# Turning the operands of fp32 split products: weights stationary, 256 tokens moving, in a two-layer decoder trunk

## The chip, the core and the metric

The kernel runs on one core of a Trainium2 chip. The core has TensorE (matmuls, results only into PSUM), VectorE (DVE), ScalarE (ACT), GpSimd (POOL) and SyncE (SP), which here issues the loads. The metric is the device time of one execution, in microseconds, as the median of several runs. Before the change it is 2340.84 us (three runs, 2338.79 to 2340.88).

## The reference

256 tokens of width 2048 go through two layers, all in fp32.

```
mod = silu(c) @ ada_w + ada_b            # shift, scale, gate; six vectors of 2048 a layer
h = x * (1 + scale) + shift
layer 0: y = gated linear attention(h)   # keys, queries (1024 each), values, r (2048 each),
                                         # gate logits of rank 16, chunks of 64 tokens, 4 heads;
                                         # o = rmsnorm(o) * g * silu(r), then @ w_out
layer 1: y = stick-breaking attention(h) # q from h, k and v from x, 16 heads, then @ w_out
x = layernorm(alpha * x + (1 + gate) * y)
y = relu(h @ w1 + b1)^2 @ w2 + b2        # the MLP of both layers, 2048 -> 8192 -> 2048
x = layernorm(alpha * x + (1 + gate) * y)
```

## The kernel before

**Weights.** All weight matrices come as 768 tiles of 128 x 1024 fp32 (512 KB) in one fixed order, into a ring of four slots (`raw`). ScalarE writes the rounded high part `w_hi` (L320), DVE the rest `w_lo = raw - w_hi` (L678). The activations are split the same way, into `h_hi` and `h_lo`, with the model width on partitions and the tokens along the columns. A product is then three matmuls of the type fp32r: w_hi with h_hi (L1071), w_hi with h_lo (L1072), w_lo with h_hi (L1075). Other matmuls (attention, transposes) are plain fp32.

**Two kinds of tiles.** A *stripe* is eight tiles that hold 512 output columns and all 2048 input rows, two blocks of 128 rows in a tile. `stripe_tile` makes h the stationary operand (128 tokens) and 512 weight columns the moving one: 2 blocks x 2 token halves x 3 = 12 matmuls of 512 columns in a tile. The results stand with tokens on partitions in two PSUM banks; stripes alternate between banks 0, 1 and banks 2, 3 (`par`). The *wide* tiles (`wide`) serve the projections back to width 2048 (`go`, `d0`, `ao`, `d1`); they have 12 matmuls of 512 columns too and are not changed.

The stages in order, with their tiles: lead 24 (half of the queries and all keys of layer 0, loaded beside the first modulation rows), gq1 8 (the other queries), gv 32, gr 32, go 32, u0 128, d0 128, aq 32, ak 32, av 32, ao 32, u1 128, d1 128.

**Results turned afterwards.** Keys, queries and the MLP's hidden layer are wanted with output columns on partitions. So after a stripe ScalarE copies its two banks to `S` (`rows_out`, L344), TensorE transposes them in eight blocks of 128 x 128 into banks 6 and 7 (`turn`, L1109), and ScalarE (`relu` L357, `keep_turned` L365) or DVE (`gla_keys`, `gla_queries`) takes them from there. DVE squares the relu's result (L956). A new stripe waits until the copy of the stripe before the last is done (`rows_copied`).

**Order.** Nothing is scheduled by the hardware. Each engine's block is a list of tiles, and a hook table `H[tile]` says which small operations follow which tile; the loops of the MLPs pass their hooks by tile number within two stripes. ScalarE and DVE split tile t as soon as slot t - 4 has been used, so they can be up to three tiles ahead of TensorE.

**Modulation vectors.** 200 + 24 rows of 128 x 2048 weights (1 MB) are multiplied on DVE with the broadcast silu(c) and summed (L683), spread over the stages.

**Gate rows.** The residual (L742, L743) multiplies y, which has tokens on partitions, with 1 + gate along the columns, the same for all partitions. `gate_column` makes the gate as a 128 x 16 column block; `gate_spread` (L1144) transposes each of its columns, broadcast to 128 x 128, so that 16 transposes make the rows in PSUM, eight at a time; `gate_rows` (L412) copies them to `G`. This happens four times.

**The gate of r.** silu(r) is built from functions of one table set: on ScalarE Abs (L541), Exp, Ln and Exp, on DVE two operations between and after them, then `o_gate` multiplies o with it. Heads of o go through the same two banks 4 and 5 one after another (`o_head`, L1232).

**Stage ends.** Before the next stage DVE adds the residual, makes mean and variance and normalises; TensorE transposes X (L1122) to make the next h.

Of the kernel before, what the change touches and what calls it, by code (L numbers as in the profile page):

```python
# [66 lines left out]
STRIPE0 = {"gv": 4, "u0": 8, "aq": 24, "ak": 28, "av": 32, "u1": 36}  # L67
TURNED0 = {"u0": 4, "aq": 20, "ak": 24, "u1": 28}
# [8 lines left out]

GLAO_AT = [T0["gr"] + i for i in (24, 25, 26, 27, 31)] + [T0["go"] + i for i in (0, 7, 8)]
# [5 lines left out]
def build_kernel(nc, tiles, mods, c_t, x_rows, mod_b, ln_t, b1_t, bg_t, w_gl, wgu, normg_t, ln_rows, b2_rows, out):  # L84
# [3 lines left out]
    with ctx:  # L88
# [55 lines left out]
        gla_rows = [rows_buf, G[:, 0:TW], G[:, TW:2 * TW], rows_buf]  # L144
# [27 lines left out]
        rows_copied, blocks_turned = sem("rows_copied"), sem("blocks_turned")  # L172
        turned_act, turned_dve, squared = sem("turned_act"), sem("turned_dve"), sem("squared")
        src_hi, src_lo = sem("src_hi"), sem("src_lo")
        g_made, g_spread, g_copied = sem("g_made"), sem("g_spread"), sem("g_copied")
# [5 lines left out]
        r_ln, r_log, r_sig, part_done = sem("r_ln"), sem("r_log"), sem("r_sig"), sem("part_done")  # L181
# [4 lines left out]

        block = ctx.enter_context(nc.Block())

        def h_bank(occ, pr):
            return {H_GLAO: 6 + pr % 2, H_KV: 4 + pr % 2}.get(occ, 4 + pr % 4)  # L190

# [66 lines left out]
        def _(pool):  # L258
# [35 lines left out]

            pool.wait_ge(h_lo_ready, PAIRS * (H_GLAO + 1))
            load_rows(0)
            load_b2(0)
            pool.wait_ge(tile_used, T0["d0"] + 128)
            load_rows(1)
            pool.wait_ge(a_exp, SB_H // 2)  # L300
            load_rows(2)
            load_b2(1)
            pool.wait_ge(tile_used, T0["d1"] + 64 + 32)
# [4 lines left out]
        def _(act):  # L308
# [30 lines left out]
            def rows_out(done, par, dst, s=None):  # L339
                def f():  # L340
                    act.wait_ge(tile_used, done)
                    if s is not None:
                        act.wait_ge(blocks_turned, s)
                    nc.scalar.activation(dst, ps[:, 2 * par:2 * par + 2, :], ACT.Copy).then_inc(rows_copied, 1)  # L344
                return f
# [16 lines left out]
            def keep_turned(s, dst, scale=1.0):  # L362
                def f():
                    act.wait_ge(blocks_turned, s + 1)
                    nc.scalar.activation(dst, ps[:, 6:8, :].rearrange("p a n -> p (a n)"), ACT.Copy, scale=scale)\  # L365
                      .then_inc(turned_act, 1)
                return f
# [38 lines left out]
            def gate_rows(occ, r):  # L406
                def f():
                    bank = GATE_BANK[occ]
                    if occ == 0:
                        act.wait_ge(blocks_turned, N_GLA_TURNED)  # L410
                    act.wait_ge(g_spread, 2 * occ + r + 1)
                    nc.scalar.activation(G[:, r * TW:(r + 1) * TW], ps[:, bank:bank + 2, :].rearrange("p a n -> p (a n)"), ACT.Copy)\  # L412
                      .then_inc(g_copied, 1)
                return f
# [81 lines left out]
            rows3 = lambda v: v.rearrange("p (a n) -> p a n", a=TOK)  # L496

            for j, (bank, dst) in enumerate(((2, gla_rows[1]), (0, gla_rows[0]), (4, gla_rows[2]))):
                def f(j=j, bank=bank, dst=dst):
                    act.wait_ge(tile_used, K - LEAD_TILES + j + 1)  # L500
                    nc.scalar.activation(rows3(dst), ps[:, bank:bank + 2, :], ACT.Copy).then_inc(rows_copied, 1)
                H[K + j].append(f)
            for at, f in ((4, gate_log), (5, gate_log2), (6, gate_log3), (9, decays1), (10, decays2), (12, decays3)):
                H[K + at].append(f)
            H[K + 14].append(rows_out(K + 8, 1, rows3(gla_rows[3]), 1))
# [10 lines left out]
            def o_squares(h):  # L516
                def f():
                    act.wait_ge(o_done, h + 1)
                    for tok in range(TOK):
                        link(nc.scalar.activation(o_junk, ps[:, 4 + tok, :], ACT.Square, accum_out=ssq[:, 2 * h + tok:2 * h + tok + 1]))  # L520
                return f

            def o_out(h):
                def f():
# [3 lines left out]
                    for tok in range(TOK):  # L528
                        ins = nc.scalar.activation(gO[:, tok, h * GLA_DV:(h + 1) * GLA_DV], ps[:, 4 + tok, :], ACT.Identity,
# [4 lines left out]
            def r_abs(i):  # L534
                def f():
# [3 lines left out]
                    else:  # L539
                        act.wait_ge(blocks_turned, N_GLA_TURNED)  # L540
                    link(nc.scalar.activation(staged(), ps[:, 2 * (i % 2):2 * (i % 2) + 2, :], ACT.Abs))  # L541
                return f

            def r_exp(i):
                return lambda: link(nc.scalar.activation(rows_buf, rows_buf, ACT.Exp, scale=-1.0))

            def r_log1p(i):
                return lambda: nc.scalar.activation(rows_buf, rows_buf, ACT.Ln, bias=1.0).then_inc(r_ln, 1)

            def r_gate(i):  # L550
                def f():
                    act.wait_ge(r_log, i + 1)
                    nc.scalar.activation(rows_buf, rows_buf, ACT.Exp).then_inc(r_sig, 1)
                return f

            for h in range(GLA_H):
                B = RR + 8 * h
                for at, f in ((7, o_squares), (8, o_out), (11, r_abs), (12, r_exp), (13, r_log1p), (15, r_gate)):
# [907 lines left out]
```

## Time and profile before

| | |
|---|---|
| median of three runs | 2340.84 us (2338.79 to 2340.88) |
| the profiled execution | 2337.4 us |
| its span | 2335.6 us |
| instructions in the span | 31124 |
| TensorE busy | 2264.4 us, 97% of the span |
| DVE busy | 1753.2 us, 75% |
| ScalarE busy | 1142.1 us, 49% |
| mean DMA rate | 280 GB/s |
| mean granted TensorE clock | 0.985 of full speed |

Busy shares are averages over stages with different limits. Matmuls overlap in the records: a record of 0.39 us can start every 0.23 us, so the time that a matmul costs is read from start to start or from the chain of waits, not from its mean. A weight load (PEld) is a record of its own beside the matmuls. The span runs from the first instruction to the last; the execution's own time holds 1.8 us more.

### The profile page before, as it was taken

Reading aid. Unit: us, or ns where it says so; the run is one execution under the profiler, and the core shown is the slowest. Engines: PE = TensorE matmul, PEld = TensorE weight load, DVE = VectorE, ACT = ScalarE, POOL = GpSimd, SP = SyncE. Lnnn points to the kernel's source line nnn. Section 1 sums busy time; section 2 is a strip of 40 time slices with the busy share of each in tenths; the row PEclk is TensorE's granted clock in tenths of the full one; section 3 lists DMA queues with packets and bytes.
Section 4 is the critical chain, followed back from the end, with each engine's and each line's share of the span. In section 5 each row is a group of like instructions: output and inputs, shape, how many; then the busy total and the mean of one; then the engine's idle time right before and its main releaser. Section 6 shows DMA issues by size and latency. Waiting matters only on the chain.

```text
span 2335.6 us, 31124 instructions
## 1 busy us (share of the span) xinstructions
PE 2264.4 (97%) x10288; PEld 1863.1 (80%) x10288; DVE 1753.2 (75%) x1679; ACT 1142.1 (49%) x1379; POOL 14.5 (1%) x34
## 2 busy tenths in 40 slices
PE   5799999999999999999999999999999999999997
PEld 3578878778888888888878888887888888888886
DVE  6989788897777788898896975679765445556656
ACT  3354466364444555444455555545444445444442
POOL 1000000000000000000000000000000000000000
PEclk8899999999999999999999999999999999999999
DMA  9979888879888888979978865676776555666563
GB/s 388 399 295 364 330 323 303 322 286 340 332 314 331 322 337 336 337 255 349 339 297 309 303 249 198 251 286 236 273 281 220 188 180 180 212 193 191 196 227 125
DMA packets 145689, 653.91 MB, mean 280 GB/s; under 512 B 16400, under 2 KB 16656, under 8 KB 115520
## 3 DMA queue, kind: packets, MB, share of 16 engines
q1 hardware_dynamic: 144000, 642.05, 75.2%
q0 software_dynamic: 1600, 10.69, 1.2%
q8 instruction: 54, 0.88, 0.2%
q14 instruction: 35, 0.29, 0.0%
HBM read 650.57 MB, written 2.10 MB: 279 GB/s over the span
## 4 chain that ended last, share of the span: by engine, by line
PE 90%; DVE 5%; DMA 2%; issue 1%; ACT 0%; SPq 0%; DVEq 0%; ACTq 0%
PE ps L1071 28%; PE ps L1072 28%; PE ps L1075 28%; DMA R<-in_mods 2%; PE ps L1109 2%; DVE w_lo L678 1%; PE ps L1122 1%; DVE mod_w L683 1%; DMA mod_w<-in_mods 1%; DVE X L743 1%; DVE stats L745 0%; DVE S L742 0%; PE ps L1216 0%; PE ps L1232 0%; DVE R L683 0%
## 5 line engine op out<-in xcount | busy, mean ns | idle before, releaser
L678 DVE TENSOR_TENSOR w_lo<-raw,w_hi 128x1024 fp32r<-128x1024 f32 x768 | 934.4, 1222 | 530.0 <-ACT w_hi L320 500.8
L1071 PE MATMUL ps<-w_hi,h_hi 128*128 128x512 f32 x3072 | 1216.5, 396 | 0.0
L1072 PE MATMUL ps<-w_hi,h_lo 128*128 128x512 f32 x3072 | 1204.0, 392 | 0.0
L320 ACT ACTIVATE w_hi<-raw 128x1024 fp32r<-128x1024 f32 x768 | 810.2, 1059 | 756.9 <-PE ps L1075 680.0
L1075 PE MATMUL ps<-w_lo,h_hi 128*128 128x512 f32 x3072 | 828.7, 390 | 2.3 <-DVE w_lo L678 2.3
L1071 PEld LDWEIGHTS ps<-w_hi,h_hi 128*128 128x128 f32 x3072 | 581.9, 189 | 125.9 <-issue 5.5
L1075 PEld LDWEIGHTS ps<-w_lo,h_hi 128*128 128x128 f32 x3072 | 578.2, 188 | 124.7 <-DVE w_lo L678 3.1
L1072 PEld LDWEIGHTS ps<-w_hi,h_lo 128*128 128x128 f32 x3072 | 581.9, 189 | 118.6 <-issue 0.7
L683 DVE SCALAR_TENSOR_TENSOR mod_w<-mod_w,cs 128x2048 f32<-128x2048 f32 x200 | 456.7, 2284 | 14.1 <-ACT cs L436 8.4
L976 DVE TENSOR_TENSOR h_lo<-R,h_hi 128x512 fp32r<-128x512 f32 x128 | 87.6, 684 | 10.7 <-ACT h_hi L588 10.7
L357 ACT ACTIVATE S<-ps,b1t 128x256 f32<-128x256 f32 x128 | 50.2, 475 | 85.5 <-PE ps L1109 85.5
L588 ACT ACTIVATE h_hi<-R 128x512 fp32r (+1 forms) x128 | 78.7, 615 | 0.0
L344 ACT ACTIVATE S<-ps 128x1024 f32<-128x1024 f32 x41 | 42.2, 1028 | 65.1 <-PE ps L1075 64.4
L447 ACT ACTIVATE R<-R,coef 128x256 f32<-128x256 f32 x16 | 8.7, 593 | 76.7 <-DVE coef L838 76.7
L1194 PE MATMUL ps<-R 128*16 128x256 f32 x32 | 11.7, 506 | 34.5 <-DVE h_lo L819 34.5
L1109 PEld LDWEIGHTS ps<-ident,S 128*128 128x128 f32 x336 | 39.2, 140 | 5.5
L1109 PE MATMUL ps<-ident,S 128*128 128x128 f32 x336 | 43.5, 272 | 0.0
L683 DVE SCALAR_TENSOR_TENSOR R<-R,cs 128x2048 f32<-128x2048 f32 x16 | 36.5, 2286 | 7.4 <-DMA R<-in_mods 7.4
L956 DVE TENSOR_TENSOR R<-S 128x1024 f32 (+1 forms) x32 | 39.0, 1218 | 0.0
L1122 PE MATMUL ps<-ident,X 128*128 128x128 f32 x160 | 25.7, 304 | 13.1 <-DVE X L756 12.2
L381 ACT ACTIVATE S<-ps,coef 128x256 f32<-128x256 f32 x64 | 32.3, 555 | 10.2 <-PE ps L1122 7.7
L1122 PEld LDWEIGHTS ps<-ident,X 128*128 128x128 f32 x160 | 21.4, 157 | 18.0 <-DVE X L756 13.8
(146 smaller groups left out, 629.9 us busy)
## 6 DMA issues: line engine op xcount, KB each, us to landing
raw<-in_tiles SPq DMA_DIRECT2D x768, 512.0 KB, 4.4
mod_w<-in_mods SPq DMA_DIRECT2D x200, 1024.0 KB, 6.7
R<-in_mods SPq DMA_DIRECT2D x16, 1024.0 KB, 10.8
R<-in_ln_rows POOLq DMA_DIRECT2D x8, 1024.0 KB, 8.1
G<-in_mods SPq DMA_DIRECT2D x4, 1024.0 KB, 10.7
S<-in_mods SPq DMA_DIRECT2D x4, 1024.0 KB, 12.7
X<-in_x_rows SPq DMA_DIRECT2D x1, 2048.0 KB, 11.2
S<-in_b_rows POOLq DMA_DIRECT2D x2, 1024.0 KB, 7.5
```

Source lines behind the costliest of these rows:

```text
L320: nc.scalar.activation(w_hi[:, slot, :], raw[:, slot, :], ACT.Copy).then_inc(hi_ready, 1)
L344: nc.scalar.activation(dst, ps[:, 2 * par:2 * par + 2, :], ACT.Copy).then_inc(rows_copied, 1)
L357: ins = nc.scalar.activation(turned_buf[:, blk * SEQ:(blk + 1) * SEQ], ps[:, 6 + blk // 2, (blk % 2) * SEQ:(blk % 2 + 1) * SEQ], ACT.Relu, ...
L588: nc.scalar.activation(h_hi[:, slot:slot + 2, :], R[:, bass.ds(kt * SEQ, 2 * SEQ)].rearrange("p (a t) -> p a t", a=2), ACT.Copy).then_inc( ...
L678: nc.vector.tensor_tensor(w_lo[:, slot, :], raw[:, slot, :], w_hi[:, slot, :].bitcast(F32), ALU.subtract)\
L683: nc.vector.scalar_tensor_tensor(buf, buf, 1.0, cs[:], ALU.mult, ALU.mult, accum_out=mod_t[:, bass.ds(a, 1)]).then_inc(mod_done, 1)
L976: nc.vector.tensor_tensor(h_lo[:, slot:slot + 2, :], R[:, bass.ds(kt * SEQ, 2 * SEQ)].rearrange("p (a t) -> p a t", a=2), h_hi[:, slot:slo ...
L1071: mm(dst, h_hi[:, kt, toks], w_hi[:, slot, c], start=start, stop=False, skip_group_check=more)
L1072: return mm(dst, h_lo[:, kt, toks], w_hi[:, slot, c], start=False, stop=False, skip_group_check=more)
L1075: return mm(dst, h_hi[:, kt, tok * P:(tok + 1) * P], w_lo[:, slot, c], start=False, stop=stop, skip_group_check=more)
L1109: last = nc.tensor.transpose(ps[:, 6 + blk // 2, o:o + P], rows[:, tok * SW + blk * P:tok * SW + (blk + 1) * P], ident[:])
L1122: last = nc.tensor.transpose(ps[:, h_bank(occ, pr), i * SEQ + tok * P:i * SEQ + (tok + 1) * P], src[:, tok, kt * P:(kt + 1) * P], ident[:])
```

## The change

- A new `turned_tile` takes the place of `stripe_tile` for the lead, gq1, u0, aq, ak and u1 (352 tiles). The stationary operand is a block of 128 weight columns, the moving one h with all 256 tokens: 2 row blocks x 4 column blocks x 3 = 24 matmuls of 256 columns in a tile. Results stand with output columns on partitions, four blocks of 256 tokens in the same two banks.
- `turn` and the copies ahead of it are gone; relu and `keep_turned` read the stripe's own banks after `tile_used`, one step in place of two. Keys and queries of layer 0 are copied once and read by DVE from `S` and `G`. A stripe waits for `turned_act` of the stripe two before in place of `rows_copied`. DVE's squares move from tiles 15 and 7 to tiles 13 and 5.
- `gate_spread` and `gate_rows` are gone. `gate_turn` makes one transpose of the 128 x 16 block, ScalarE copies the 16 x 128 result, POOL stores it in DRAM and loads it back broadcast to all partitions (`spread_gate`). The residual waits for that load.
- The gate of r is one Silu, with the other table loaded again afterwards. The o products move from tiles 3, 11, 19, 27 of stage gr to tiles 3, 5, 8, 10 and alternate between two pairs of banks.
- values, r and the wide tiles keep their products.

```diff
+            def turned_tile(t, j, par, inputs=None, slot=None, bank=None):
+                pe.wait_ge(hi_ready, t + 1)
+                if inputs is not None:
+                    pe.wait_ge(h_lo_ready, inputs)
+                slot = j % RING if slot is None else slot
+                bank = 2 * par if bank is None else bank
+                parts = [(2 * (j % ST) + i, ps[:, bank + blk // 2, (blk % 2) * SEQ:(blk % 2 + 1) * SEQ],
+                          slice(i * SW + blk * P, i * SW + (blk + 1) * P), blk % 2 == 0) for i in range(2) for blk in range(SW // P)]
+
+                for kt, dst, c, clears in parts:
+                    mm(dst, w_hi[:, slot, c], h_hi[:, kt, :], start=kt == 0 and clears, stop=False, skip_group_check=True)
+                    mm(dst, w_hi[:, slot, c], h_lo[:, kt, :], start=False, stop=False, skip_group_check=True)
+                pe.wait_ge(lo_ready, t + 1)
+                for kt, dst, c, _ in parts:
+                    last = mm(dst, w_lo[:, slot, c], h_hi[:, kt, :], start=False, stop=kt == KT - 1, skip_group_check=True)
+                last.then_inc(tile_used, 1)
...
-            def relu(s, i, layer, first=False):
+            def relu(done, par, i, layer, first=False):
                 def f():
-                    act.wait_ge(blocks_turned, s + 1)
+                    act.wait_ge(tile_used, done)
                     if not (first and layer == 0):
                         act.wait_ge(squared, 16 * layer + i)
                     for blk in range(4):
                         col = 64 * layer + 4 * i + blk
-                        ins = nc.scalar.activation(turned_buf[:, blk * SEQ:(blk + 1) * SEQ], ps[:, 6 + blk // 2, (blk % 2) * SEQ:(blk % 2 + 1) * SEQ],
+                        ins = nc.scalar.activation(turned_buf[:, blk * SEQ:(blk + 1) * SEQ],
+                                                   ps[:, 2 * par + blk // 2, (blk % 2) * SEQ:(blk % 2 + 1) * SEQ],
                                                    ACT.Relu, bias=b1t[:, bass.ds(col, 1)])
...
+            def gate_turn(occ):
+                def f():
+                    pe.wait_ge(g_made, occ + 1)
+                    if occ == 0:
+                        pe.wait_ge(o_copied, 3)
+                    elif occ != 2:
+                        pe.wait_ge(turned_act, TURNED0["u0" if occ == 1 else "u1"] + 16)
+                    nc.tensor.transpose(ps[0:KT, GATE_BANK[occ], 0:P], g_col[:], ident[:]).then_inc(g_turned, 1)
...
+            def spread_gate(occ):
+                pool.wait_ge(g_kept, occ + 1)
+                pool.dma_start(g_rows[occ, :, :], G[0:KT, 0:P]).then_inc(g_stored, 16)
+                pool.wait_ge(g_stored, 16 * (occ + 1))
+                pool.dma_start(G[:].rearrange("p (k n) -> p k n", k=KT), g_rows[occ, :, :].unsqueeze(0).to_broadcast([P, KT, P]))\
+                    .then_inc(g_loaded, 16)
...
-                stripes(up, u, occ, hooks(0, first=True))
+                stripes(up, turned_tile, lambda k: None, occ, {j: [f] for j, f in enumerate(rest)})
                 with pe.Fori(1, 8) as b:
-                    stripes(up + BODY * b, u + 2 * b, None, hooks(b))
+                    stripes(up + BODY * b, turned_tile, lambda k: pe.wait_ge(turned_act, s + 2 * b + k - 1), None, {})
...
+O_AT = [T0["gr"] + i for i in (3, 5, 8, 10)]
+SILU_AT = [T0["gr"] + i for i in (16, 19, 27, 35)]
...
+                    nc.scalar.activation(staged(), ps[:, 2 * (i % 2):2 * (i % 2) + 2, :], ACT.Silu).then_inc(r_taken, 1)
```

## Rows read from the trace of the kernel before

**Rows 1.** The page, its part on the chain that ended last: shares of the span.
```profile
PE 90%; DVE 5%; DMA 2%; issue 1%; ACT 0%; SPq 0%; DVEq 0%; ACTq 0%
PE ps L1071 28%; PE ps L1072 28%; PE ps L1075 28%; DMA R<-in_mods 2%; PE ps L1109 2%; DVE w_lo L678 1%; PE ps L1122 1%; DVE mod_w L683 1%; DMA mod_w<-in_mods 1%; DVE X L743 1%; DVE stats L745 0%; DVE S L742 0%; PE ps L1216 0%; PE ps L1232 0%; DVE R L683 0%
```
**Rows 2.** Waits of the whole run: who for whom, us in total, times, longest.
```profile
ACT w_hi L320 <- PE ps L1075: 680.0, 494, 3.4
...
PE ps L1194 <- DVE h_lo L819: 34.5, 8, 13.2
...
PE ps L1075 <- DVE w_lo L678: 2.3, 2, 1.4
```
**Rows 3.** Waits of SyncE's queue, 487 to 851 us.
```profile
SPq L211 <- DVE w_lo L678: 267.9, 125, 4.8
```
**Rows 4.** Stretches: length, busy us (instructions) of PE, PEld, DVE, ACT, POOL, clock, DMA, GB/s.
```profile
0.00:143.00 143.00, 101.33 (x371) 71.97 (x372) 115.64 (x121) 51.59 (x70) 9.18 (x24) 0.86 0.96 378
...
258.00:354.00 96.00, 96.00 (x421) 76.52 (x420) 77.72 (x71) 56.21 (x74) 0.00 (x0) 1.00 0.92 349
...
487.00:851.00 364.00, 364.00 (x1672) 302.59 (x1671) 289.72 (x254) 176.43 (x214) 0.00 (x0) 1.00 0.86 324
```
**Rows 5.** Chain of waits, 555 to 601 us: start, us, what.
```profile
562.31 0.91 PE ps L1075 x4
...
565.03 0.91 PE ps L1075 x4
...
576.82 0.87 PE ps L1109 x8
...
599.50 0.87 PE ps L1109 x8
```
**Rows 6.** Groups by line, TensorE, shapes apart: busy us, mean ns, idle before.
```profile
L1109 PE MATMUL ps<-ident,S 128*128 128x128 f32 x336 | 43.5, 272 | 0.0
...
L1144 PE MATMUL ps<-ident,g_col 128*128 128x128 f32 x64 | 8.3, 272 | 0.0
...
L1109 PE MATMUL ps<-ident,G 128*128 128x128 f32 x16 | 2.1, 272 | 0.0
```
**Rows 7.** Chain of waits, 1436.5 to 1440.5 us, two attention products of heads.
```profile
1437.37 0.43 PE ps L1375 x2
1437.81 0.22 PE ps L1376 x2
```
**Rows 8.** Groups by line, weight loads, shapes apart.
```profile
L1376 PEld LDWEIGHTS ps<-R 128*128 128x128 f32 x32 | 6.1, 189 | 0.8
```
**Rows 9.** Instructions in order of time, all engines, 1363.2 to 1363.6 us.
```profile
1363.22 0.19 PEld L1071 LDWEIGHTS ps<-w_hi,h_hi 128*128 128x128 f32 x1
...
1363.33 0.19 PEld L1072 LDWEIGHTS ps<-w_hi,h_lo 128*128 128x128 f32 x1
...
1363.56 0.39 PE L1072 MATMUL ps<-w_hi,h_lo 128*128 128x512 f32 x1
```
**Rows 10.** TensorE in order of time, 61.2 to 63.4 us, slow clock at first.
```profile
61.24 0.63 PE L1071 MATMUL ps<-w_hi,h_hi 128*128 128x512 f32 x1
61.67 0.63 PE L1072 MATMUL ps<-w_hi,h_lo 128*128 128x512 f32 x1
```
**Rows 11.** TensorE in order of time, last products before a stop (69.49 to 73.86 us).
```profile
69.26 0.61 PE L1075 MATMUL ps<-w_lo,h_hi 128*128 128x512 f32 x2
```
**Rows 12.** TensorE in order of time, 1437 to 1440 us.
```profile
1436.76 0.61 PE L1075 MATMUL ps<-w_lo,h_hi 128*128 128x512 f32 x2
```
**Rows 13.** ScalarE in order of time, 577.77 to 600.45 us, relu of one stripe.
```profile
577.91 1.57 ACT L357 ACTIVATE S<-ps,b1t 128x256 f32<-128x256 f32 x4 [2.72 <-PE ps L1109]
```
**Rows 14.** Stretches, one stripe of the up projection of layer 0.
```profile
577.77:600.45 22.68, 22.68 (x106) 18.84 (x104) 17.30 (x16) 10.87 (x13) 0.00 (x0) 1.00 0.86 322
```
**Rows 15.** ScalarE in order of time, 0 to 14 us.
```profile
0.80 1.28 ACT L429 ACT_TABLE_LOAD   x1 [0.80 <-PEq L1456]
```
**Rows 16.** The page, DMA issues: count, KB each, us to landing.
```profile
R<-in_ln_rows POOLq DMA_DIRECT2D x8, 1024.0 KB, 8.1
```

More of the change, by code:

```diff
@@ L539, in f @@
                     else:
[L540 to L553, printed above, removed]
+                        act.wait_ge(turned_dve, N_GLA_TURNED)
+                    nc.scalar.activation(staged(), ps[:, 2 * (i % 2):2 * (i % 2) + 2, :], ACT.Silu).then_inc(r_taken, 1)
                 return f
             for h in range(GLA_H):
[L557 to L561 removed]
+                H[O_AT[h] + 4].append(o_squares(h))
+                H[O_AT[h] + 5].append(o_out(h))
+                H[SILU_AT[h]].append(r_silu(h))
+            H[SILU_AT[GLA_H - 1] + 1].append(lambda: nc.scalar.preload_act_table_set("natural_log_exp_and_others"))
+            H[RR + 17].append(gate_row_out(0))
             for pr in range(PAIRS):
@@ L569, in mlp @@
             def mlp(layer):
-                up, down, s = T0[f"u{layer}"], T0[f"d{layer}"], TURNED0[f"u{layer}"]
+                up, down = T0[f"u{layer}"], T0[f"d{layer}"]
                 def hooks(b, first=False):
                     i, t = 2 * b, up + BODY * b
-                    late = {10: [rows_out(t + 8, 0, staged(), s + i)], 14: [relu(s + i, i, layer, first)]}
-                    early = {2: [rows_out(t, 1, staged(), s + i - 1)], 6: [relu(s + i - 1, i - 1, layer)]}
+                    late = {11: [relu(t + 8, 0, i, layer, first)]}
+                    early = {3: [relu(t, 1, i - 1, layer)]}
                     return late if first else {**late, **early}
@@ L599, in mlp @@
                     t = down + 64 * half
-                    extra = {2: [rows_out(down, 1, staged(), s + 15)], 6: [relu(s + 15, 15, layer)],
-                             12: [gate_rows(1 + 2 * layer, 0)], 15: [gate_rows(1 + 2 * layer, 1)]} if half == 0 else {}
+                    extra = {3: [relu(down, 1, 15, layer)], 12: [gate_row_out(1 + 2 * layer)]} if half == 0 else {}
                     body(t, src_hooks(t, 0, extra, made=4))
@@ L997, in mlp @@
                     if half == 0:
-                        extra = {7: [square(15)], 8: [lambda: gate_column(1 + 2 * layer, f"g_m{layer}")]}
+                        extra = {5: [square(15)], 8: [lambda: gate_column(1 + 2 * layer, f"g_m{layer}")]}
                     else:
@@ L1091, in _, with stripes @@
             H = defaultdict(list)
-            def stripes(t, u, occ=None, hooks=None):
+            def stripes(t, tile, free, occ=None, hooks=None):
                 for j in range(BODY):
                     if j % ST == 0:
-                        pe.wait_ge(rows_copied, u + j // ST - 1)
-                    stripe_tile(t + j, j, j // ST, None if occ is None or j >= ST else PAIRS * occ + j + 1)
+                        free(j // ST)
+                    tile(t + j, j, j // ST, None if occ is None or j >= ST else PAIRS * occ + j + 1)
@@ L1198, in _ @@
                     t = LEAD_TILES * pr + i
-                    stripe_tile(t, pr, None, slot=t % RING, bank=bank)
+                    turned_tile(t, pr, None, slot=t % RING, bank=bank)
             def gates():
@@ L1324, in _ @@
                 H[Q + j].append(f)
[L1325 to L1329 removed]
+            H[Q + 18].append(gate_turn(2))
             def turn_kv(pr):
@@ L1383, in _ @@
                 H[HEAD_AT[p]].append(head_part(p))
-            for i in range(6):
-                stripes(Q + BODY * i, u + 2 * i, {0: H_Q, 2: H_KV}.get(i))
+            for i in range(4):
+                stripes(Q + BODY * i, turned_tile, lambda k, s=TURNED0["aq"] + 2 * i: pe.wait_ge(turned_act, s + k - 1), {0: H_Q, 2: H_KV}.get(i))
+            stripes(V, stripe_tile, lambda k: pe.wait_ge(turned_act, TURNED0["ak"] + 3 + k))
+            stripes(V + BODY, stripe_tile, lambda k: pe.wait_ge(rows_copied, STRIPE0["av"] + 1 + k))
             heads = lambda j: (head_lo, j // 2 + 1)
```

175 lines of the change are left out of this document (59 added, 116 removed).

## The prediction

> **What bounds the kernel now.** I read the chain of waits first: it is 90% TensorE, and three lines of split products (L1071, L1072, L1075) hold 28% each [rows 1]. Then the waits, for what feeds it late. Over the whole run matmuls wait 34.5 us for h_lo, all of it in the lead, and for the weights' low part (w_lo) only 2.3 us; ScalarE waits 680 us for TensorE, so it runs ahead [rows 2]. In the up projection of layer 0 alone SyncE waits 267.9 us for a free slot before it loads, so loads run ahead too [rows 3]. The stretches show TensorE busy all of 258 to 354 us and 487 to 851 us, DVE at 80% [rows 4]. Outside the lead (0 to 143 us, where loads rule) and the four stage ends, time is therefore the sum of TensorE's instructions. The chain gives their prices [rows 5]. Four split products take 0.91 us, 0.2267 each; 12 of them are one tile, which repeats at 2.72 us (562.31 to 565.03). A stripe of 8 tiles and one group of eight transposes repeats at 22.68 (576.82 to 599.50); 8 x 2.72 = 21.76 leaves 0.92 us for the group, of which its own piece is 0.87.
>
> **Transposes of results: removed.** 336 + 16 = 352 of them [rows 6], 44 groups: 4 in the GLA part, 32 in the MLPs, 8 for queries and keys. None lies in the lead. 44 x 0.92 = 40.5 us off the path.
>
> **Gate rows: 64 transposes of a broadcast column [rows 6] become 4 of a 128x16 block.** Eight groups of 0.92, less four single transposes at about 0.15 (an eighth of 0.87, and the 0.05 that a change of kind takes around a group): 7.4 - 0.6 = 6.8 us.
>
> **The turned product decides.** A tile had 12 products of 512 moving columns; it gets 24 of 256, each with a weight load of its own. The columns streamed are the same, the instructions double. The trace has no split product of 256 columns, so neighbours bound it.
> - Weight load. Two plain fp32 matmuls of 128 columns, each with a load of 128, take 0.22 us, 0.11 each, though a load's record lasts 189 ns [rows 7, 8]: such a load repeats every 0.11 us and hides beside the other's stream. Two loads of split products stood 0.11 apart as well (1363.22, 1363.33), and from the first of them to the second product are 0.34 us, 0.227 of which is the first product: 0.11 to 0.115 [rows 9]. That is just about half of 0.2267.
> - Stream. At 2.4 GHz 512 columns would be 213.3 ns; the chain has 226.7, so 13.3 over. At a granted clock of 1.2 GHz they step by 0.43 (61.24, 61.67), which is 512 / 1.2 with nothing over [rows 10]. Plain fp32 of 256 columns takes 0.43 for two, 0.215 each, two passes of 106.7 with 2 ns over [rows 7]. So 13 ns arise only where 4-byte columns stream at the full rate. If they belong to the stream (a rate limit of 16/17), 256 columns cost 113.3; if to the instruction, 106.7 + 13.3 = 120.0. The last two products before a stop, the very last with no load behind it, make a record of 0.61 us [rows 11]; two with a load behind them also 0.61 [rows 12]. So the next load isn't what stretches them.
> I take the stream: 113.3, a tile of 24 x 0.1133 = 2.72 us as before, cost zero. The ends are 0.109 (an eighth of a group, 0.87) and 0.124 (rival C).
> The Trainium skill (TensorE: Matmul & The Clock Gate, section Back-to-back issue gap) has a rule against the change: a warm matmul lasts N/2.4 plus about 2.5 ns, the latter for each instruction whatever its size. By that 12 more instructions a tile cost 0.03 us. The rule gives 215.8 for 512 columns where the row has 226.7, so it is not the whole price of a split product; what it would do here is rival G.
>
> **Eviction.** A copy of the stripe, then relu from turned banks, becomes one relu (four pieces, 1.57 us [rows 13]) straight from the stripe's banks. ScalarE has 10.87 us of a stripe's 22.68 [rows 14]: nothing on the path. A stripe now waits until the stripe two before is evicted; that comes after tile 3 of the one between, 4 tiles (11 us) ahead: nothing. With that cover gone each stripe would pay the 1.57.
>
> **DVE, DMA.** A stripe shrinks to 21.76 us; DVE has 17.30 in it [rows 14], 80%, with the square now two tiles earlier. The up projection moved 324 GB/s and would ask for 338; 349 was held at 258 to 354 us [rows 4]. Nothing; at worst the pace stays and its 16 groups, 14.7 us, are lost (rival D).
>
> **Silu gate.** Per head Abs, Exp, Ln, Exp on ScalarE and two DVE operations become one Silu. It needs another table, so two loads at 1.28 each [rows 15]. ScalarE is busy 56 of 96 us there [rows 4] and TensorE doesn't wait for it. Nothing; uncovered, 2.6 us. The o products of heads 1 to 3 come earlier, in banks of their own: the same instructions. Their squares and scalings (about 3 us a head) now fall into ScalarE's tiles 7 to 15 of the stage, 12 + 9 splits of 1.1 = 22 us against 24.5 of TensorE, which waits for the second head's at the earliest 3 tiles later.
>
> **Gate rows by DRAM.** POOL issues an 8 KB store and a broadcast load of 1 MB, each behind the copy out of PSUM. The nearest 1 MB load on that queue takes 8.1 us [rows 16]; I double it for store and wait: 16. Readers come 39 tiles (106 us) later in the GLA part and over 50 later elsewhere. Behind them in POOL's queue stand only the norm and bias rows, due a stage later. Nothing.
>
> **Lead.** Its 24 tiles are turned too, beside loads; the products wait there [rows 2]. Nothing. The stage ends keep their chain.
>
> **Sum.** The profiled execution took 2337.4 us (span 2335.6 and 1.8 around it): 2337.4 - 40.5 - 6.8 = 2290.1. The median of the runs shown, 2340.84, is 3.4 above it: 2294.
>
> **Rivals.**
> - *B, the 13.3 ns are paid per instruction.* 24 x 0.120 = 2.88, 0.16 more a tile, on 328 tiles (352 turned less 24 in the lead) +52.5; less 47.3 is +5.2: 2346, slower. The change loses from 113.3 + 47300 / (328 x 24) = 119.3 ns a product. For it: 226.67 ns are exactly 256 + 16 ticks of 1.2 GHz as well as 17/16 of 256. Against: [rows 10 to 12]. Chance 0.26.
> - *C, the weight load doesn't hide.* If the 13.3 come on top of a load of 0.11, a product takes 0.124: +0.26 a tile, +84, net +37: 2378. Against: the fp32 pairs [rows 7], but those stream their columns at half the rate. 0.11.
> - *D, loads or DVE hold the up projection of layer 0 at its pace*: 14.7 less: 2308. Against: [rows 3]. 0.08.
> - *E, at 256 columns the excess vanishes*: 0.109, a tile 2.62, 34 us more: 2260. For it only the fp32 pairs. 0.05.
> - *G, a small fixed part beside the rate.* If 2.5 of the 226.7 are per instruction, as fp32 has 2 over, 256 columns take 112.1 + 2.5 = 114.6: 0.03 a tile, +10: 2304. 0.17.
>
> **Numbers.** The forecast holds 0.33, 2294, its own range 2286 to 2302. Such timing tells 0.2%, 4.7 us. Faster: 0.33 + 0.17 + 0.08 + 0.05 = 0.63. B lies at the line (2342 to 2350 with its joins): 0.11 as same, 0.15 as slower; with C slower is 0.26. The range leaves out E and C and holds B: 2280 to 2352.
>
> **What would show it.** Turned products in the up projection starting every 113 ns (mine), 115 (G), 120 (B), 124 (C) or 109 (E); its 16 tiles in 43.5 us, in B 46.1; no transposes between stripes; down projections unchanged at 2.72 us a tile; TensorE busy throughout with waits for w_lo of a few us. A gap ahead of each stripe, products waiting for w_lo, or a residual waiting for G would show me wrong elsewhere.

## The result

The changed kernel takes 2343.56 us (median of 20 runs, 2341.40 to 2346.41); the kernel before took 2338.81 beside it (20 runs, 2336.15 to 2343.18). The ratio is 1.0018 [1.0011, 1.0025]: 4.7 us slower (2.6 to 5.8), a small amount, but clear of the noise. The forecast was 2294. The time is that of rival B (2346, net +5.2), and the turned products start every 120 ns, which is B's price.

The profiled execution took 2341.98 us, with a span of 2340.3. The chain of waits, by engine and by line, answers to [rows 1]. L1056, L1057 and L1060 are the old products of 512 moving columns; L1086, L1087 and L1090 are the turned ones of 256 (w_hi with h_hi, w_hi with h_lo, w_lo with h_hi).

```profile
PE 87%; DVE 7%; DMA 3%; issue 2%; ACT 0%; SPq 0%; DVEq 0%; ACTq 0%
PE ps L1060 15%; PE ps L1056 15%; PE ps L1057 15%; PE ps L1086 13%; PE ps L1087 13%; PE ps L1090 13%; DVE w_lo L683 2%; DMA R<-in_mods 2%; DVE mod_w L688 1%; DMA mod_w<-in_mods 1%; PE ps L1111 1%; DMA raw<-in_tiles 1%; DVE X L748 1%; DVE S L747 1%; DVE stats L750 1%
```

The waits of the whole run (who for whom, us in total, times, longest) answer to [rows 2]. ScalarE still waits for TensorE, not the other way round; TensorE's waits for h_lo and w_lo are as before in sum; the new wait of POOL for its own DRAM store is 4 x 4 us, and no engine is listed as waiting for the broadcast behind it.

```profile
ACT w_hi L338 <- PE ps L1090: 476.7, 301, 2.1
...
PE ps L1181 <- DVE h_lo L824: 33.2, 8, 12.8
...
POOL G L306 <- DMA g_rows<-G: 16.4, 4, 5.3
...
PE ps L1060 <- DVE w_lo L683: 1.7, 2, 1.4
```

SyncE in the up projection of layer 0, 487 to 851 us, answers to [rows 3]: its wait for a free slot has grown from 267.9 to 272.1, so loads still run ahead.

```profile
SPq L218 <- DVE w_lo L683: 272.1, 125, 4.1
```

The stretches answer to [rows 4] and [rows 14] (length, busy us and instructions of PE, PEld, DVE, ACT, POOL, clock, DMA, GB/s). In the second, the up projection, TensorE's recorded products went from 1672 to 2987 and DVE's load fell a little. TensorE is busy all 364 us of it, and all 96 us of the first. The last of the four rows, in the part of layer 0 after the lead, bears on the chain above, whose DVE share grew from 5% to 7%: over these 48 us the chain runs through DVE, which is busy 47.90 of them, as much as in the kernel before, yet TensorE is busy 47.88. DVE comes close to setting the pace there, and costs TensorE under 1 us.

```profile
258.00:354.00 96.00, 96.00 (x409) 75.34 (x408) 73.76 (x66) 52.53 (x77) 1.05 (x2) 1.00 0.93 360
487.00:851.00 364.00, 364.00 (x2987) 361.87 (x2987) 283.85 (x248) 160.01 (x195) 0.53 (x1) 1.00 0.85 319
577.77:600.45 22.68, 22.68 (x191) 22.68 (x190) 17.30 (x15) 9.57 (x13) 0.00 (x0) 1.00 0.87 320
160.00:208.00 48.00, 47.88 (x241) 40.31 (x240) 47.90 (x49) 24.27 (x23) 0.00 (x0) 1.00 0.86 324
```

The chain of 555 to 603 us (start, us, what) answers to [rows 5]. A piece of eight turned products is 0.96 us, 0.120 each; tiles repeat at 2.88 (555.62 to 558.50), and 16 tiles take 46.08 (555.62 to 601.70) with no transposes between them.

```profile
555.62 0.96 PE ps L1090 x8
...
558.50 0.96 PE ps L1090 x8
...
601.70 0.96 PE ps L1090 x8
```

Groups by line, shapes apart (busy us, mean ns, idle before), answer to [rows 6]. The 352 transposes of results are gone; the 32 of the gated o rows, which the change doesn't touch, are left, and the gate column is turned four times in one piece.

```profile
L1086 PE MATMUL ps<-h_hi,w_hi 128*128 128x256 f32 x2816 | 703.8, 287 | 0.0
...
L1133 PE MATMUL ps<-ident,g_col 128*16 128x128 f32 x4 | 1.1, 271 | 0.0
```

TensorE in order of time, 60.5 to 72 us, answers to [rows 10]. While the clock is at 1.2 GHz turned products start 0.21 us apart (61.97, 62.18), which is 256 / 1.2 = 213 ns with nothing over; at 2.4 GHz they start 0.12 apart (64.07, 64.19), which is 13.3 over 106.7.

```profile
61.97 0.41 PE L1086 MATMUL ps<-h_hi,w_hi 128*128 128x256 f32 x1
62.18 0.41 PE L1087 MATMUL ps<-h_lo,w_hi 128*128 128x256 f32 x1
...
64.07 0.28 PE L1087 MATMUL ps<-h_lo,w_hi 128*128 128x256 f32 x1
64.19 0.28 PE L1086 MATMUL ps<-h_hi,w_hi 128*128 128x256 f32 x1
```

ScalarE in order of time has the relu of a stripe, 1.56 us as in [rows 13]; the page's DMA issues have the broadcast of the gate row, beside [rows 16].

```profile
586.38 1.56 ACT L373 ACTIVATE S<-ps,b1t 128x256 f32<-128x256 f32 x4
```

```profile
G<-g_rows POOLq DMA_DIRECT2D x4, 1024.0 KB, 7.6
```

Where the time went can be read by parts, since each part ends with TensorE's wait for the first norm of the next. These are the first such wait at each of the three ends, from TensorE in order of time:

```profile
462.07 1.09 PE L1111 MATMUL ps<-ident,X 128*128 128x128 f32 x8 [2.24 <-DVE X L761]
...
1191.74 1.09 PE L1111 MATMUL ps<-ident,X 128*128 128x128 f32 x8 [2.26 <-DVE X L761]
...
1599.19 1.49 PE L1111 MATMUL ps<-ident,X 128*128 128x128 f32 x8 [2.26 <-DVE X L761]
```

In the trace of before the same transposes start at 467.59, 1193.45 and 1598.73 us. Rival B's terms, put against each part (0.16 for each turned tile, 0.92 for each group, 1.7 for each gate row):

| part | before, us | after, us | difference | by B's terms |
|---|---|---|---|---|
| lead and GLA | 467.6 | 462.1 | -5.5 | 8 x 0.16 - 3.7 - 1.7 = -4.1 |
| MLP of layer 0 | 725.9 | 729.7 | +3.8 | 128 x 0.16 - 14.7 - 1.7 = +4.1 |
| attention | 405.3 | 407.5 | +2.2 | 64 x 0.16 - 7.4 - 1.7 = +1.1 |
| MLP of layer 1 and the end | 736.9 | 741.1 | +4.2 | +4.1 |
| span | 2335.6 | 2340.3 | +4.7 | +5.2 |

Single parts of two executions also differ by TensorE's clock, which was granted at 1.2 GHz in different stretches. The first two rows are from the trace of before, the third from that of after; the granted clock is the number before the last two.

```profile
131.00:134.40 3.40, 3.40 (x9) 2.62 (x9) 3.40 (x4) 2.08 (x3) 0.00 (x0) 0.51 0.56 171
148.10:151.50 3.40, 3.40 (x9) 2.64 (x9) 3.40 (x3) 1.92 (x1) 0.00 (x0) 0.50 0.69 287
131.00:134.40 3.40, 3.37 (x24) 2.71 (x25) 3.17 (x3) 3.30 (x5) 0.00 (x0) 1.00 0.25 77
```

In these stretches the kernel before starts its products 0.43 us apart in place of 0.23, which costs it an estimated 3.3 us; both lie shortly after the waits of the lead; the changed kernel runs at full clock in both (24 and 30 products). From TensorE's last wait for h_lo on (129.81 before, 131.03 after) to the end of the part, the kernel before takes 337.8 us and the changed one 331.0, 6.7 less. B's terms for that stretch come to -3.6 (-4.1, and +0.5 for the three tiles of the lead that fall into it). The 3.1 us that are left are what the slow clock took from the kernel before. At the start of the attention part it is the other way round: from 1193 to 1201 us the mean granted clock is 0.79 before and 0.57 after. So these parts can test the terms to an us or two, not more closely.

### The profile page after: what moved, and what is told of

It is laid out like the page before. It is cut to its first block, busy times and chain, and to the rows that moved or that the text cites. A ratio compares the mean times of both kernels' runs of the same rounds, so it can differ in the third digit from the quotient of the medians.

```text
span 2340.3 us, 38554 instructions
## 1 busy us (share of the span) xinstructions
PE 2270.1 (97%) x14100; PEld 2042.6 (87%) x14100; DVE 1746.5 (75%) x1671; ACT 1091.1 (47%) x1325; POOL 18.6 (1%) x42
## 4 chain that ended last, share of the span: by engine, by line
PE 87%; DVE 7%; DMA 3%; issue 2%; ACT 0%; SPq 0%; DVEq 0%; ACTq 0%
PE ps L1060 15%; PE ps L1056 15%; PE ps L1057 15%; PE ps L1086 13%; PE ps L1087 13%; PE ps L1090 13%; DVE w_lo L683 2%; DMA R<-in_mods 2%; DVE mod_w L688 1%; DMA mod_w<-in_mods 1%; PE ps L1111 1%; DMA raw<-in_tiles 1%; DVE X L748 1%; DVE S L747 1%; DVE stats L750 1%
## 5 line engine op out<-in xcount | busy, mean ns | idle before, releaser
L1086 PE MATMUL ps<-h_hi,w_hi 128*128 128x256 f32 x2816 | 703.8, 287 | 0.0
L1087 PE MATMUL ps<-h_lo,w_hi 128*128 128x256 f32 x2816 | 699.5, 285 | 0.0
L1056 PE MATMUL ps<-w_hi,h_hi 128*128 128x512 f32 x1664 | 652.0, 392 | 0.0
L1057 PE MATMUL ps<-w_hi,h_lo 128*128 128x512 f32 x1664 | 647.8, 389 | 0.0
L1086 PEld LDWEIGHTS ps<-h_hi,w_hi 128*128 128x128 f32 x2816 | 547.8, 195 | 6.2 <-issue 5.4
L1087 PEld LDWEIGHTS ps<-h_lo,w_hi 128*128 128x128 f32 x2816 | 547.9, 195 | 0.0
L1060 PE MATMUL ps<-w_lo,h_hi 128*128 128x512 f32 x1664 | 450.6, 389 | 1.8 <-DVE w_lo L683 1.7
L1090 PE MATMUL ps<-h_hi,w_lo 128*128 128x256 f32 x2816 | 395.9, 283 | 0.0
L1060 PEld LDWEIGHTS ps<-w_lo,h_hi 128*128 128x128 f32 x1664 | 312.0, 188 | 68.4 <-DVE w_lo L683 3.5
L1056 PEld LDWEIGHTS ps<-w_hi,h_hi 128*128 128x128 f32 x1664 | 312.5, 188 | 66.0 <-issue 1.2
L1057 PEld LDWEIGHTS ps<-w_hi,h_lo 128*128 128x128 f32 x1664 | 312.5, 188 | 64.8 <-issue 1.0
L1090 PEld LDWEIGHTS ps<-h_hi,w_lo 128*128 128x128 f32 x2816 | 364.2, 192 | 0.0
L373 ACT ACTIVATE S<-ps,b1t 128x256 f32<-128x256 f32 x128 | 49.8, 471 | 0.0
L1181 PE MATMUL ps<-R 128*16 128x256 f32 x32 | 12.4, 531 | 33.2 <-DVE h_lo L824 33.2
```

The source lines that it names most:

```text
L1056: mm(dst, h_hi[:, kt, toks], w_hi[:, slot, c], start=start, stop=False, skip_group_check=more)
L1057: return mm(dst, h_lo[:, kt, toks], w_hi[:, slot, c], start=False, stop=False, skip_group_check=more)
L1060: return mm(dst, h_hi[:, kt, tok * P:(tok + 1) * P], w_lo[:, slot, c], start=False, stop=stop, skip_group_check=more)
L1086: mm(dst, w_hi[:, slot, c], h_hi[:, kt, :], start=kt == 0 and clears, stop=False, skip_group_check=True)
L1087: mm(dst, w_hi[:, slot, c], h_lo[:, kt, :], start=False, stop=False, skip_group_check=True)
L1090: last = mm(dst, w_lo[:, slot, c], h_hi[:, kt, :], start=False, stop=kt == KT - 1, skip_group_check=True)
```

## The experiments

**One product at a time.** Chains of 32 products, one kind after the other, show whether the 13.3 ns go with the columns or with the instruction. This program was executed once, like the two further ones of its kind below. The pieces (the loops around them and three other pieces are left out; the remarks at the ends are added):

```python
mm(ps[:, 1, :], W[:, w(i)], M[:, 0:512], **opts(i))               # L65, fp32r
mm(ps[:, 2, 0:384], W[:, w(i)], M[:, 0:384], **opts(i))           # L67
mm(ps[:, 3, 0:256], W[:, w(i)], M[:, 0:256], **opts(i))           # L69
mm(ps[:, 4, 0:256], W[:, w(0)], M[:, 0:256], **opts(i))           # L71, same stationary block
mm(ps[:, 5, 0:256], X[:, 0, w(i)], X[:, 1, 0:256], **opts(i))     # L73, fp32, 64 instructions
mm(ps[:, 6, 0:256], Wb[:, w(i)], Mb[:, 0:256], **opts(i))         # L75, bf16
mm(ps[0:64, 1, 0:256], W[:, w(i, 64)], M[:, 0:256], **opts(i))    # L79, 64 stationary columns
mm(ps[0:64, 2, :], W[:, w(i, 64)], M[:, 0:512], **opts(i))       # L81, 64 stationary columns
mm(ps[:, 3, 0:256], W[0:64, w(i)], M[0:64, 0:256], **opts(i))     # L83, 64 rows
mm(ps[:, 4, 0:128], W[:, w(i)], M[:, 0:128], **opts(i))           # L85, 128 columns
```

> A kernel of nothing but runs of 32 back-to-back products, one kind after another, each product with a stationary operand of its own unless said (its output is not the reference's, it computes none of the trunk). The trace after has split products of 256 columns at 120 ns where 512 take 226.7, so my rate theory (17/16 of the column time, 113.3) has fallen. Three theories for the 13.3 ns over the column time. T1, a fixed part of each fp32r product, whatever its width and its load: 512, 384, 256 columns at 226.7, 173.3, 120.0; 120.0 also with the same stationary block every time, with 64 stationary columns, and with 64 rows; 512 with 64 stationary columns 226.7. T2, the weight load adds it (128 columns of load): with 64 stationary columns 113.3 at 256 and 220 at 512. T3, at 256 columns the load sets the pace, not the stream: 384 at 173 but 256 with 64 stationary columns clearly under 113. For all: bf16 of 256 at 107 to 110 and of 512 at 214 to 217, fp32 of 256 at 216. fp32r of 128 columns: T1 says 66.7 unless a load of 0.11 holds it; T3 says 110 to 120.

Measured, its chain of waits (start, us, what):

```profile
33.18 7.25 PE ps L65 x32
40.44 5.57 PE ps L67 x32
46.01 3.83 PE ps L69 x32
49.84 3.84 PE ps L71 x32
53.68 13.82 PE ps L73 x64
67.49 3.49 PE ps L75 x32
...
77.89 3.65 PE ps L79 x32
81.54 7.36 PE ps L81 x32
...
92.93 3.72 PE ps L85 x32
```

Divided by 32, a product of 512 columns takes 226.6 ns, of 384 it takes 174.1 (settled steps 173.3), of 256 it takes 119.7 (settled 120.0). The part over N/2.4 is 13.3 ns at each of the three sizes: it belongs to the instruction, and the rate of 16/17 is refuted (by it 384 columns would take 170.0 and 256 columns 113.3). A stationary block that stays the same doesn't help (L71, 120.0), nor do 64 rows in place of 128 (settled steps 120). The trace has a weight load beside every product, also where the block stays the same (32 loads for the 32 products of L71), so "the instruction" here means a product with its load: no run separates the two.

bf16 of 256 columns takes 109.1. Plain fp32 takes 216 ns for each of the two instructions that one product becomes (64 for 32 products); that holds for the attention products of [rows 7] as well. 128 columns of a split product take 111 to 112, so there the repeat is set by something else than the columns (53.3); the two loads of [rows 9] stood as far apart. With 64 stationary columns a product of 256 takes 113.3 once settled, as T2 has it, but one of 512 (L81) takes 230 and not T2's 220; nor does 113.3 come clearly under 113, as T3 would.
The Trainium skill's rule of N/2.4 plus 2.5 (TensorE: Matmul & The Clock Gate, Back-to-back issue gap) agrees with bf16 in both sizes (109.1 of 109.2; starts 215.8 apart at 512 columns) and doesn't hold for the split products, which have 10.8 ns more at either size.

**The side edits alone.** The kernel before, with the gate rows by DRAM, the Silu gate and the earlier o products, and nothing turned:

```diff
-                    act.wait_ge(g_spread, 2 * occ + r + 1)
-                    nc.scalar.activation(G[:, r * TW:(r + 1) * TW], ps[:, bank:bank + 2, :].rearrange("p a n -> p (a n)"), ACT.Copy)\
+                    act.wait_ge(g_turned, occ + 1)
+                    nc.scalar.activation(G[0:KT, 0:P], ps[0:KT, GATE_BANK[occ], 0:P], ACT.Copy).then_inc(g_kept, 1)
...
+                    nc.scalar.activation(staged(), ps[:, 2 * (i % 2):2 * (i % 2) + 2, :], ACT.Silu).then_inc(r_taken, 1)
```

> Before, with only the small parts of the change: gate rows by one transpose and DRAM, Silu for r, o products in two pairs of banks; the stripes and their transposes stay as before. By my sum the gate rows give 6.8 us and the rest nothing: 2338.8 - 6.8 = 2332. A rival, that the small parts cost something which the turned products have not paid (the change measured +4.8 where 120 ns a product gives +52.5 - 40.5 = +12.0 for the turned part, so the small parts must give about 7): if they gave nothing, this would be 2339.

Measured: 2330.50 us beside 2339.55, ratio 0.9960 [0.9947, 0.9974], 9 us off where 6.8 were expected (the interval is 6.1 to 12.4, which holds it). ScalarE is busy 50.9 of the 96 us in which it had 56.2 [rows 4]. By subtraction the turned part alone is +0.58% of the time, 13.6 us (about 10 to 17 by the two intervals); its terms are 52.5 - 40.5 = 12.0.

**Half-width products without a turn.** The kernel before, h stationary as ever, with each 512-column product of the stages in question cut into two of 256 (the products of w_lo in the same way; `w` is 256 there):

```diff
                 for kt, tok, c in parts:
-                    times_hi(ps[:, bank + tok, :], kt, tok, slot, c, kt == 0, more=True)
+                    for n in range(SW // w):
+                        times_hi(ps[:, bank + tok, n * w:(n + 1) * w], kt, tok, slot, slice(c.start + n * w, c.start + (n + 1) * w), kt == 0 and n == 0, more=True)
```

> Before, with h stationary as ever, but every product of the stages that the change turns (lead, gq1, u0, u1, aq, ak; 352 tiles) made as two of 256 moving columns; transposes, copies and gate rows as before. It separates the width from the orientation. If the fixed part is paid per product, whatever is stationary: 24 x 120.0 = 2.88 us a tile against 2.72, +0.16 on 328 tiles, +52.5: 2391. If the 120 ns belong to weights being the stationary operand (a new block of w for each pair, h from four buffers), two halves cost as much as one whole here: 2339.

Measured: 2386.50 us, ratio 1.0197 [1.0182, 1.0213], 47 us slower (42.6 to 49.8), short of the 52.5 by about a tenth. Its chain in the up projection has the price again:

```profile
561.29 0.96 PE ps L1075 x8
...
582.41 0.87 PE ps L1112 x8
...
606.31 0.87 PE ps L1112 x8
```

Part of what is missing can be read here. A stripe repeats at 23.90 us (582.41 to 606.31), which is 8 x 2.88 and 0.86 for the group of transposes, where it was 0.92 before. In the kernel before, the products of 512 columns behind the group at 576.82 step by 228, 234, 236, 224, 231, 236, 228, 233 and 230 ns until they are at 227 (behind the group at 599.50 only by 232 and 231), while those of 256 columns here keep to 117 to 120 from the second on. Over some 40 groups that is 2 us, an estimate. It leaves 50.5 against an interval that ends at 49.8; for the rest no run gives the cause.

So the orientation has no part in it: here h is stationary as before, and the same columns in twice the instructions have the turned products' price. The transposes that the turn saves (40.5 us) and the side edits bring the changed kernel back near zero.

**What a load leaves over.** The 113.3 ns with 64 stationary columns suggested that the left-over part grows with the stationary block (16 ticks of 1.2 GHz for 128 columns, T2). This varies that width (the first five of ten pieces, and their rows):

```python
mm(ps[0:32, 1, 0:256], W[:, w(i, 32)], M[:, 0:256], **opts(i))        # L65
mm(ps[0:64, 2, 0:256], W[:, w(i, 64)], M[:, 0:256], **opts(i))        # L67
mm(ps[0:96, 3, 0:256], W[:, w(i, 96)], M[:, 0:256], **opts(i))        # L69
mm(ps[:, 4, 0:256], W[:, w(i)], M[:, 1024:1280], **opts(i))           # L71
mm(ps[0:32, 5, :], W[:, w(i, 32)], M[:, 0:512], **opts(i))            # L73
```

> Again nothing but runs of back-to-back fp32r products (no trunk is computed). The run before had 226.7 at 512 columns, 173.3 at 384, 120.0 at 256 (also with one stationary block throughout), but 113.3 at 256 with 64 stationary columns. T2, a load of c columns takes c/8 ticks of 1.2 GHz from the stream that it runs beside: at 256 moving columns 110.0 with 32 stationary, 113.3 with 64, 116.7 with 96, 120.0 with 128, wherever the moving block lies; at 512 with 32 216.7, with 64 220; at 384 with 64 166.7; 512 and 256 alternating (a pair) 346.7. T1, the part is fixed per product: 120, 120, 120 at 256 for 32, 64, 96, which the 113.3 already speaks against. T4, load and stream meet in a pattern of their own that a quiet rate settles into (512 with 64 stationary columns had 230, and did not settle): then widths at 64 and 32 columns are irregular, and 512 with 64 is again near 230 rather than 220. 192 columns with a load of 128: 93.3 by T2 alone, 111 if the load's own rate holds it.

```profile
33.49 3.77 PE ps L65 x32
37.26 3.63 PE ps L67 x32
40.89 3.71 PE ps L69 x32
44.61 3.83 PE ps L71 x32
48.44 7.40 PE ps L73 x32
```

256 moving columns with 32, 64, 96 and 128 stationary ones take 117.8, 113.3, 116.0 and 120.0 ns (117.8 as 3.77 / 32): no straight line. 512 columns with 32 take 231.3 and with 64 again 230, both more than the 226.7 with 128; 384 with 64 take 173.3, as with 128. Alternating products of 512 and 256 columns take 353.3 ns a pair, where fixed parts would give 346.7; 192 columns take 111.7. T2 fell, and T1 (13.3 for each instruction) holds for 256, 384 and 512 columns where all of a run have one size and 128 stationary columns. What is left is T4, irregular sizes without a rule.

**Pair the halves.** If the instruction is what costs, the turned tile can have fewer: h_hi and h_lo lie side by side and move as 512 columns past one w_hi block. A tile is 8 products of 512 and 8 of 256. The two halves of a bank are then added by DVE, after ScalarE has put the bias to one; a stripe takes four banks in place of two, so two stripes take all eight. Only the two up projections do so; the rest is as in the changed kernel.

```diff
+                for kt, bank, c in parts:
+                    mm(ps[:, bank, :], w_hi[:, slot, c], h_both[:, kt, :, :].rearrange("p a t -> p (a t)"), start=kt == 0, stop=False, skip_group_check=True)
+                pe.wait_ge(lo_ready, t + 1)
+                for kt, bank, c in parts:
+                    last = mm(ps[:, bank, 0:SEQ], w_lo[:, slot, c], h_hi[:, kt, :], start=False, stop=kt == KT - 1, skip_group_check=True)
...
+                        nc.vector.tensor_tensor(four, ps[:, 4 * par:4 * par + 4, 0:SEQ], four, ALU.add).then_inc(y_made, 1)
```

> The kernel after, with the up projections (u0, u1, 256 tiles) changed: w_hi is stationary once and h_hi and h_lo stand side by side as 512 moving columns, two results of 256 in one bank; w_lo takes h_hi alone. 8 products of 512 and 8 of 256 in a tile in place of 24 of 256; ScalarE takes the one half with the bias, DVE adds the other and squares (one DVE operation of 1.2 us more in a stripe, 80% to 86% of it). By the load theory (16 ticks a load): 8 x 226.7 + 8 x 120.0 = 2.773 us a tile against 2.880, -0.107 x 256 = -27.3 from 2343.6: 2316. If the pace were set by columns alone, 2343; if DVE or the bank waits bound it, above 2325.

Measured: 2321.92 us, ratio 0.9925 [0.9911, 0.9938]. The chain in the up projection:

```profile
590.34 1.84 PE ps L1103 x8
592.17 0.95 PE ps L1106 x8
593.13 1.84 PE ps L1103 x8
```

The tile is 2.79 us (590.34 to 593.13), 0.09 less than the turned one, on 256 tiles 23 us; the ratios differ by 0.93%, 21.8 us. Most of the 5.9 us above the expected time are the eight wide products: 230 ns each and not 226.7, 0.02 on a tile, 5 on 256. DVE, which got the additions, is busy 311 of the 364 us of that stretch and TensorE waits for it once, 0.7 us.

**The parts that pay, together.** The side edits, the paired tiles in the two up projections, and the old stripes with their transposes in the GLA and attention parts:

```diff
+                        ins = nc.scalar.activation(turned_buf[:, blk * SEQ:(blk + 1) * SEQ], ps[:, 4 * par + blk, SEQ:2 * SEQ],
+                                                   ACT.Identity, bias=b1t[:, bass.ds(col, 1)])
...
-                H[t + 10].append(rows_out(t + 8, i % 2, staged(), TURNED0["aq"] + i))
+                H[t + 10].append(rows_out(t + 8, i % 2, staged(), N_GLA_TURNED + i))
```

> e2 (small parts of the change, stripes turned afterwards) with the pairs of e5 in u0 and u1 alone; lead, gq1, aq and ak keep 12 products of 512 and the transposes, 2.72 + 0.115 = 2.835 us a tile against 2.880 turned. From 2330.5: 256 x (2.835 - 2.773) = -15.9: 2315. Against e5 it should gain 0.045 x 72 = 3 us; if DVE's extra operation costs anything it costs it in both.

Measured: 2318.81 us, ratio 0.9913 [0.9897, 0.9928]: the lowest of all, 20 us under the kernel before. It is 3.1 us below the run above, as expected, but the two intervals overlap. The 3.8 us above the expected 2315 are again what the wide products of the pairs have too much (0.02 x 256 = 5). Against the side edits alone it is 0.47% or 11 us less, and its terms are 32 groups x 0.92 = 29.4 saved and 256 x 0.07 = 17.9 paid.

**The sizes between, and a change of size.** This asks how far the fixed 13.3 ns reach, and why the paired tile's wide products take 230:

```python
mm(ps[:, 1, 0:448], W[:, w(i)], M[:, 0:448], **opts(i))               # L65
mm(ps[:, 2, 0:320], W[:, w(i)], M[:, 0:320], **opts(i))               # L67
mm(ps[:, 3, 0:288], W[:, w(i)], M[:, 0:288], **opts(i))               # L69
mm(ps[0:112, 4, 0:256], W[:, w(i, 112)], M[:, 0:256], **opts(i))      # L71
mm(ps[0:80, 5, 0:256], W[:, w(i, 80)], M[:, 0:256], **opts(i))        # L73
# six rounds of 8 x 512 (L76) and 8 x 256 (L78), then of 8 x 512 (L81) and 4 x 512 (L83)
```

> Not the trunk: chains of split products (fp32r) that read one converted block, with results that nobody uses. It tests how the 13.3 ns over the columns' time go with the number of columns and with the stationary block's width. T1 (a fixed 13.3 ns for each product, if the stationary block has 128 columns): 448 columns 200.0 ns, 320 columns 146.7, 288 columns 133.3, 256 columns 120.0. The rate theory (17/16 of the columns' time) would give 198.3, 141.7, 127.5 and 113.3. 256 moving columns with a stationary block of 112 and of 80 columns: T2 (an eighth of the stationary width, in ticks of 1.2 GHz, is left over) 118.3 and 115.0; T1 120.0 for both; T4 (a pattern without a rule that I know) something between 112 and 120. Blocks of 8 products of 512 columns followed by 8 of 256: by T1 8 x 226.7 = 1.813 us and 8 x 120.0 = 0.960 us, 2.773 for the sixteen; by T4, as in the paired tile, 1.84 and 0.95, 2.79. Twelve products of 512 without a change of size: 2.720 by either, the tile of the kernel before.

```profile
33.09 6.49 PE ps L65 x32
39.58 4.70 PE ps L67 x32
44.27 4.21 PE ps L69 x32
48.48 3.63 PE ps L71 x32
52.12 3.63 PE ps L73 x32
55.75 1.84 PE ps L76 x8
57.59 0.95 PE ps L78 x8
58.54 1.84 PE ps L76 x8
...
75.25 1.81 PE ps L81 x8
...
77.97 1.81 PE ps L81 x8
```

448, 320 and 288 columns take 202.8, 146.9 and 131.6 ns, 16.1, 13.5 and 11.6 over N/2.4: the rate theory (198.3, 141.7, 127.5) is off by 4 to 5 each time, T1's 13.3 holds at 320 and is missed by 2 to 3 at the others (448 and 288 step in a repeated pattern, 199, 207, 202, 203, 202 and 131, 131, 130, 135). The paired tile is reproduced with nothing else running (55.75 to 58.54 = 2.79), and so is the old one (75.25 to 77.97 = 2.72). After a switch from 256 to 512 columns the steps are 233, 236, 228, 233, 231 and only then 227: the switch costs what the paired tile has too much. Stationary blocks of 112 and 80 columns take 113.4 like those of 64, so neither theory of the width holds: 64, 80 and 112 columns agree, 128 take 6.7 more, and 32 and 96 lie between.

## Why the prediction was wrong

**What bounds the kernel** was read rightly: outside the lead the time is the sum of TensorE's instructions, before and after, and no other engine, load or queue took over (rival D: SyncE's wait grew; DVE comes near it from 160 to 208 us and costs under 1 us).

**The step that failed** is the price of the turned product: "I take the stream: 113.3, a tile of 24 x 0.1133 = 2.72 us as before, cost zero." It is 120.0, in the changed kernel, in the half-width kernel and alone. On 328 tiles the missing 6.7 ns x 24 are 52.5 us, and 2294 + 52.5 = 2346.5 against the measured 2343.6. The choice was between two accounts of one number, 13.3 ns over 512 columns, for which the trace of before had no second size; what was taken as evidence for the stream was none:
- [Rows 10], the slow clock with nothing over, was taken to tie the 13 ns to the rate of the columns. The changed kernel's turned products have nothing over at 1.2 GHz as well (213 ns), and 13.3 at 2.4 GHz. The excess vanishes at the slow clock at both sizes, so the row couldn't tell the two apart.
- [Rows 11] and [rows 12], a stop without and with a load behind, compare records that hold one step between two products, with the second's load in both, and then the last product's own length (0.61 = 0.227 + 0.39; alone it has a record of 0.39 at 512 columns, 0.28 at 256). They ruled out that the following load stretches a product, which B doesn't need: a part that each instruction pays for itself leaves both records alike.
- The coincidence named for B (16 ticks for each product) was worth as much as that named for the rate. Equal chances for both (0.295 each) would have left "faster" the likelier side; only evidence for B could have turned it.
- Such evidence was there. Plain fp32 has three sizes in the trace of before: 0.109 us at 128 moving columns (0.87 / 8, [rows 5]), 0.215 at 256 (0.43 / 2, [rows 7]) and 0.43 at 512 (the row below), which is 2 to 3 ns over 106.7, 213.3 and 426.7 each time. Its excess doesn't grow with the columns. The prediction used this for the size of G's fixed part, not for the choice between stream and instruction. It was a hint and no proof, since plain fp32 streams its columns at half the rate.

```profile
280.97 2.58 PE ps L1232 x6
```

**Transposes and gate rows**: the size of both was right. The parts of the span fit the terms 0.92, 1.7 and 0.16 within 1.4 us each. The GLA part is 1.4 better than its terms: slow clock cost the kernel before some 3.3 us there that the changed one was spared, less the 1.2 us by which the changed one got its last h_lo later and 0.5 for the lead's last tiles. The side edits alone gave 9 us of an expected 6.8, which its interval holds.

**Eviction, DVE, DMA, Silu, POOL**: cost nothing, as forecast. The relu from the stripe's banks is 1.56 us and no stripe waits; POOL's wait for its store is 4.1 us each time, store and broadcast some 12 where I had allowed 16; the table loads around Silu and the earlier o products are covered (TensorE busy all 96 us).

**The rivals**: B came in as it was worked out, break-even included (120.0 is above 119.3). C, E and G named 124, 109 and 114.6 and are refuted by the 120.0. G's part for each instruction was right in kind; its size was taken from fp32, where a split product has five times as much, and the rate that it kept beside that part isn't there.

**What stays open** is why a split product has 13.3 ns over its columns where bf16 has 2.5, whether the product or its weight load takes them, why stationary blocks of 64, 80 and 112 columns have 6.7, and why 32 and 96 lie between. The runs show the sizes, not the cause.

## What to carry over

Two accounts of one measured number that differ in what they scale with can't be separated by rows that hold only that size; then a chain of the new size, measured by itself, comes before the change. Until it is there, look for another kind of instruction whose size does vary, as plain fp32 did here. For split products of 128 stationary columns the price is N/2.4 + 13.3 ns an instruction at 256, 320, 384 and 512 columns (11.6 and 16.1 over at 288 and 448), so halving the moving width cost more here (52.5 us) than the transposes that it saved (40.5). Where a swap halves the width, two products can be folded into one wide move (2.79 us a tile in place of 2.88). Small edits that ride along with a large one are to be timed alone: here they were worth 9 us and the large one cost 13.6. And before a part of one trace is compared with the same part of another, compare their granted clocks.

## What was not expected of the hardware

- The part over the columns' time vanishes at the granted clock of 1.2 GHz for 512 and for 256 columns, and is 13.3 ns for both at 2.4 GHz.
- A split product of 128 moving columns, and one of 192, repeats at 111 to 112 ns with a stationary block of 128, twice what 128 columns need. (The 0.11 of [rows 7] is no such floor: plain fp32 of 128 columns takes 109 ns, in line with its 216 at 256.)
- A run of 512-column split products that follows narrower ones has to settle: after 256 columns it steps by 233, 236, 228, 233, 231, then 227; after 384 columns (with 64 stationary) by 235, 232, 231, then 227; after the transposes of the kernel before it takes three steps or ten.
- With fewer stationary columns a wide product can take longer: 231.3 ns with 32 and 230 with 64 (7.36 / 32), 226.7 with 128.
